# Loading x and the memory also with channels in the partitions, the small vectors as one array, and the plain memory later

## The reference, cut to what matters

```
def rmsnorm(x, g):
    y = x32 * lax.rsqrt(jnp.mean(x32 * x32, axis=-1, keepdims=True) + EPS)
    return (y * g).astype(x.dtype)

mem_n = rmsnorm(mem, norm_mem)
for i in range(DEPTH):                       # DEPTH = 2
    h = rmsnorm(x, norm_mix[i])
    mkv = mem_n @ w_mem_kv[i]                # keys | values of the memory
    proj = h @ w_in_a[li]                    # i = 0: q | k | v | qm
    y_tok = windowed_gqa(q, k, v, sink_a[li])        # i = 0
    y_mem = memory_attn(qm, mk, mv)
    x = x + jnp.concatenate([y_tok, y_mem], axis=-1) @ w_out[i]
    h = rmsnorm(x, norm_ffn[i])
    gu = h @ w_gate_up[i]
    x = x + (silu(gu[..., :D_FF]) * gu[..., D_FF:]) @ w_down[i]
```

## Time and profile before

| | us |
|---|---|
| median of 3 runs (lowest to highest) | 1098.73 (1098.53 to 1102.89) |
| the profiled execution | 1095.95 |
| its span (first to last instruction) | 1094.2 |
| TensorE matmul busy in the span | 1035.4 (95%) |
| VectorE busy | 738.4 (67%) |
| ScalarE busy | 585.7 (54%) |
| GpSimd busy | 117.0 (11%) |

### The profile page before, as it was taken

One profiled execution on the slowest core, in us unless ns is written; L12 is line 12 of the kernel. 1 busy time (PEld: TensorE's weight loads), 2 busy tenths in 40 slices (PEclk: granted clock), 3 DMA queues, 4 the chain that ended last, 5 costly groups with the idle time before them and its releaser, 6 DMA issues.

```text
span 1094.2 us, 13575 instructions
## 1 busy us (share of the span) xinstructions
PE 1035.4 (95%) x5224; PEld 857.8 (78%) x5224; DVE 738.4 (67%) x985; ACT 585.7 (54%) x834; POOL 117.0 (11%) x161
## 2 busy tenths in 40 slices
PE   6997899999999989899999999997989999999996
PEld 5876778789888777788888777886777788888885
DVE  4667774666446577578888766679776766777753
ACT  5557663444345567544443454576656466666641
POOL 1013121000000022200000011013540000000001
PEclk9998999999999999999999989999999999999998
DMA  9655369755565431389989786535365526564541
GB/s 335 202 155 86 106 199 263 244 176 180 166 210 187 152 124 44 114 304 351 353 324 327 288 303 212 164 120 173 125 226 188 183 91 206 178 198 164 171 138 38
DMA packets 98112, 212.42 MB, mean 194 GB/s; under 512 B 5681, under 2 KB 13313, under 8 KB 94657
## 3 DMA queue, kind: packets, MB, share of 16 engines
q1 hardware_dynamic: 93313, 194.46, 52.7%
q0 software_dynamic: 4576, 17.03, 6.4%
q10 hardware_dynamic: 160, 0.07, 0.0%
HBM read 206.82 MB, written 6.15 MB: 195 GB/s over the span
## 4 chain that ended last, share of the span: by engine, by line
PE 67%; DVE 12%; ACT 8%; DMA 5%; issue 5%; POOL 1%; SPq 1%; DVEq 0%; ACTq 0%; POOLq 0%
PE bank L867 20%; PE bank L869 20%; PE bank L868 20%; ACT hi L1191 4%; DVE lo L1619 4%; PE bank L845 3%; DMA raw<-in_w_gate_up 3%; PE bank L881 1%; PE bank L847 1%; DMA raw<-in_w_down 1%; DVE early L1450 1%; DMA raw<-in_w_in 1%; DVE xres L1493 1%; DMA small<-in_sink_a 1%; DVE big L1631 1%
## 5 line engine op out<-in xcount | busy, mean ns | idle before, releaser
L1619 DVE TENSOR_TENSOR lo<-raw,hi 128x2048 fp32r<-128x2048 f32 (+1 forms) x164 | 367.1, 2242 | 220.1 <-ACT hi L1191 219.1
L1191 ACT ACTIVATE hi<-raw 128x2048 fp32r<-128x2048 f32 (+1 forms) x164 | 303.3, 1853 | 191.9 <-PE bank L869 138.5
L867 PE MATMUL bank<-hi,xTh 128*128 128x512 f32 (+2 forms) x896 | 344.9, 385 | 3.5 <-DVE lo L1619 3.4
L869 PE MATMUL bank<-hi,xTl 128*128 128x512 f32 (+2 forms) x896 | 336.3, 375 | 0.0
L868 PE MATMUL bank<-lo,xTh 128*128 128x512 f32 (+2 forms) x896 | 336.1, 375 | 0.0
L867 PEld LDWEIGHTS bank<-hi,xTh 128*128 128x128 f32 x896 | 169.4, 189 | 35.1 <-DVE lo L1619 4.3
L869 PEld LDWEIGHTS bank<-hi,xTl 128*128 128x128 f32 x896 | 169.1, 189 | 31.4
L868 PEld LDWEIGHTS bank<-lo,xTh 128*128 128x128 f32 x896 | 169.5, 189 | 28.2
L867 PE MATMUL bank<-hi,hTh 128*128 128x512 f32 x264 | 103.5, 392 | 0.7 <-DVE lo L1619 0.7
L869 PE MATMUL bank<-hi,hTl 128*128 128x512 f32 x264 | 102.8, 389 | 0.0
L868 PE MATMUL bank<-lo,hTh 128*128 128x512 f32 x264 | 102.8, 389 | 0.0
(11 more groups left out here) (353 smaller groups left out, 1352.8 us busy)
## 6 DMA issues: line engine op xcount, KB each, us to landing
raw<-in_w_gate_up SPq DMA_DIRECT2D x44, 1024.0 KB, 5.7
raw<-in_w_down SPq DMA_DIRECT2D x30, 1024.0 KB, 5.1
raw<-in_w_ada SPq DMA_DIRECT2D x24, 1024.0 KB, 6.6
raw<-in_w_up SPq DMA_DIRECT2D x22, 1024.0 KB, 5.2
raw<-in_w_in SPq DMA_DIRECT2D x21, 1024.0 KB, 5.0
raw<-in_w_out SPq DMA_DIRECT2D x12, 1024.0 KB, 5.1
raw<-in_w_in_b SPq DMA_DIRECT2D x10, 1024.0 KB, 5.1
raw<-in_w_in_a SPq DMA_DIRECT2D x6, 1024.0 KB, 9.9
```

The costliest lines, as they stand in the source:

```text
L867: e.matmul(o, sh, h[:, k, :], start=p.first and k == 0, stop=False)
L869: done = e.matmul(o, sl, h[:, k, :], start=False, stop=p.last and k == p.nk - 1)
L1191: e.activation(hi_s[m % SPLITS][:, 0:n], raw[p.at % RAWS][:, 0:n], ACT.Copy).then_inc(hi_made, 1)
L1619: e.tensor_tensor(lo_s[s][:, 0:n], raw[p.at % RAWS][:, 0:n], hi_s[s][:, 0:n].bitcast(F), ALU.subtract).then_inc(lo_made, 1)
```

## The change

The host hands over three more arrays: `memT` and `xT`, the memory and x with channels in the partitions, and `vectors`, one array of 128 partitions by 330 numbers that holds all gains, taps, offsets, the sink logits and the slopes as columns. The rows, the gain's turn and the 8 turns of memory and x by PE are gone; ACT and DVE make `memTh`, `memTl`, `xTh` and `xTl` straight from the loaded arrays. The plain memory and the plain x are still loaded, since the squares (and later the residual) need them with tokens in the partitions. The plain memory is loaded into `xres` after the sixth weight load. The plain x goes into the same buffer and is issued by POOL behind the root of the memory's squares; the table `const` is issued there too. Both sets of squares stand behind the splits of x. The evacuation of the first `mem` tile becomes a task `late` that waits in the list, so that it comes one tile later, right before that of `vm`.

```
-MIX_TILES = [[(1024, 4, 2), (512, 4, 1), (0, 0, 1)], ...
+MIX_TILES = [[(1024, 4, [2, 2, 1]), (512, 4, [2, 2, 1]), (0, 0, 1)], ...
@@ linear
-            if p == parts - 1:
+            if p == parts - 1 and (kind, l) == ("mem", 0):
+                self.later.append(("late", t))
+            elif p == parts - 1:
                 self.evacuate(t)
@@ run
-        self.put("memgain")
         for k in range(0, 8, 2):
+            self.put("memx", k)
             self.split_through(min(k // 2, SPLITS - 1))
-            self.put("memx", k)
-        self.later.append(("memsq",))
-        self.later.append(("rows",))
-        self.later.append(("relload",))
-        for j in range(2):
-            self.pieces(0, j)
-        self.linear("mem", 0, 0, 512, len(FIRST), "mem", 2)
+        self.later.extend([("rows",), ("relload",), ("xin", 0, 0), ("xin", 0, 2), ("xin", 0, 4), ("xin", 0, 6), ("memsq",), ("sq", 0, 0), ("sq", 0, 1)])
+        self.linear("mem", 0, 0, 512, len(FIRST), "mem", [2, 1, 1, 1])
@@ ScalarE, step memx
-                    e.wait_ge(x_full, filled(step))
-                    e.wait_ge(*emptied(("memgain",)))
+                    if k == 0:
+                        e.wait_ge(d_vec, 16)
+                    e.wait_ge(d_memT[min(k // 2, 2)], 16)
                     for j in range(2):
-                        e.activation(memTh[:, k + j, :], x_bank(step)[...], ACT.Copy, scale=memgain[...])
+                        e.activation(memTh[:, k + j, :], memT[:, k + j, :], ACT.Copy, scale=col(4)[...])
@@ GpSimd
-            e.dma_start(const[:, 128:1408], a["constants"][:, 128:1408]).then_inc(d_const, 16)
-            e.dma_start(steep, a["constants"][:, 1408:1414]).then_inc(d_const, 16)
             for step in order.steps:
                 if kind == "memsq":
                     root(0, 1)
+                    e.dma_start(xres[:, :, :], a["x"][0].rearrange("(t p) d -> p t d", p=128)).then_inc(d_x, 16)
+                    e.dma_start(const[:, 128:1408], a["constants"][:, 128:1408]).then_inc(d_const, 16)
@@ SyncE
-            (memory, 4 weight loads, 16 small loads, x, then the other weights)
+            e.dma_start(memT[:, 0:2, :], a["memT"][:, 0:2, :]).then_inc(d_memT[0], 16)
+            next_load(0)
+            next_load(1)
+            e.dma_start(memT[:, 2:4, :], a["memT"][:, 2:4, :]).then_inc(d_memT[1], 16)
+            next_load(2)
+            e.dma_start(memT[:, 4:8, :], a["memT"][:, 4:8, :]).then_inc(d_memT[2], 16)
+            next_load(3)
+            e.dma_start(xT[:, 0:4, :], a["xT"][:, 0:4, :]).then_inc(d_xT[0], 16)
+            next_load(4)
+            e.dma_start(xT[:, 4:8, :], a["xT"][:, 4:8, :]).then_inc(d_xT[1], 16)
+            next_load(5)
+            e.dma_start(xres[:, :, :], a["mem"][0].rearrange("(t p) d -> p t d", p=128)).then_inc(d_mem, 16)
+            for i in range(6, len(plan)):
+                next_load(i)
```

More of the change, by code:

```diff
@@ L187, in put @@
         kind = task[0]
-        if kind in ("memgain", "rows", "rel", "columns"):
+        if kind in ("rel", "columns"):
             self.turn(task, ON_D)
@@ L248, in put @@
             self.made |= {("merged", k), ("merged", k + 1)}
+        elif kind == "late":
+            return self.evacuate(task[1])
         elif kind == "cv":
@@ L665, in build @@
             p_slots[0] = [[sb(f"p{n}0{i}", [128, 2, 256], R, sc)[:, :, :] for n in "hl"] for i in range(2)]
-        rows = early[:, 2048:2432].rearrange("p (n d) -> p n d", n=3)
-        memx = early[:, 0:2048].rearrange("p (t d) -> p t d", t=2)
-        memrow = early[0:8, 2432:2560]
+        memT = early[:, 0:2048].rearrange("p (k t) -> p k t", k=8)
+        xT = nrm[:, :, :].rearrange("p t (k n) -> p (t k) n", k=4)
         mstage = [early[:, 2560 + 512 * l:3072 + 512 * l].rearrange("p (t d) -> p t d", t=2) for l in range(2)]
@@ L771, in ready @@
             what, l = source
+            if what == "in" and l == 0:
+                return in_low, k // 2 + 1
             if what == "in":
@@ L931, in tensor_program @@
                     matmuls(parts[name[0]], name[1])
[L932 to L945, removed]
+                elif kind == "xin" and name[0]:
                     s, k = name
[L947 to L950, removed]
+                    e.wait_ge(acc_dve, order.res_at[s, k // 4])
                     turned(claim(step), blocks_of(xres, k * 128, 2))
                 elif kind == "mk":
+                    e.wait_ge(d_ident, 16)
                     t_ = order.tile_of["mem", name[0], 0]
@@ L1207, in scalar_program @@
                     gain = col((0, 2, 1, 3)[s])
-                    e.wait_ge(x_full, filled(step))
-                    e.wait_ge(*emptied(("rows",)))
+                    if s:
+                        e.wait_ge(x_full, filled(step))
+                    else:
+                        e.wait_ge(d_xT[k // 4], 16)
                     for j in range(2):
-                        e.activation(xTh[:, k + j, :], x_bank(step)[:, j * 256:(j + 1) * 256], ACT.Copy, scale=gain[:, k + j:k + j + 1]).then_inc(x_high, 1)
+                        view = x_bank(step)[:, j * 256:(j + 1) * 256] if s else xT[:, k + j, :]
+                        e.activation(xTh[:, k + j, :], view, ACT.Copy, scale=gain[:, k + j:k + j + 1]).then_inc(x_high, 1)
                 elif kind == "sq":
@@ L1654, in vector_program @@
                     gain = col((0, 2, 1, 3)[s])
-                    if s == 0 and k == 0:
-                        e.wait_ge(*emptied(("rows",)))
                     e.wait_ge(x_high, order.high_at[step])
                     for j in range(2):
-                        done = e.scalar_tensor_tensor(out=xTl[:, k + j, :], in0=x_bank(step)[:, j * 256:(j + 1) * 256], scalar=gain[:, k + j:k + j + 1],
+                        view = x_bank(step)[:, j * 256:(j + 1) * 256] if s else xT[:, k + j, :]
+                        done = e.scalar_tensor_tensor(out=xTl[:, k + j, :], in0=view, scalar=gain[:, k + j:k + j + 1],
                                                       in1=xTh[:, k + j, :].bitcast(F), op0=ALU.mult, op1=ALU.subtract)
-                    done.then_inc(x_dve, 1)
+                    done.then_inc(x_dve if s else in_low, 1)
                 elif kind == "sq":
@@ L1892, in gpsimd_program @@
                 elif kind == "relload":
-                    e.wait_ge(x_full, filled(("rows",)))
                     e.dma_start(rel, a["rel_bias_2"]).then_inc(d_rel, 16)
@@ L2048, in shape_constants @@
         c[:, 896 + 256 * t:1152 + 256 * t] = np.where(key[None, :] <= q[:, None], 0.0, -BIG)
-    c[:, 1408:1414] = [[0.125 * 2.0 ** (8.0 * (2 * k + (i >= 64) + 1) / 12) for k in range(6)] for i in range(128)]
     col, kcol = p % 64, key % 64
@@ L2054, in shape_constants, with vectors_of, turned_blocks @@
     return c
+def vectors_of(a):
+    rows = [a[n].reshape(-1, 128) for n in ("norm_mix", "norm_ffn", "norm_mem", "g_mix_2", "g_ffn_2", "c_2", "conv_rnn_w_2", "conv_rnn_b_2",
+                                            "b_rg_2", "b_ig_2", "lru_lambda_2")]
+    taps = a["conv_ffn_w_2"].reshape(-1, 128)
+    rows += [taps[0:88], a["b_in_2"][0, 2376:3400].reshape(-1, 128), taps[88:132], a["conv_ffn_b_2"].reshape(-1, 128)]
+    steep = [[0.125 * 2.0 ** (8.0 * (2 * k + (i >= 64) + 1) / 12) for k in range(6)] for i in range(128)]
+    sink = np.broadcast_to(a["sink_a"].reshape(1, 12), (128, 12))
+    return np.ascontiguousarray(np.concatenate([np.concatenate(rows).T, sink, steep], axis=1).astype(np.float32))
+def turned_blocks(x):
+    return np.ascontiguousarray(x[0].T.reshape(8, 128, 256).transpose(1, 0, 2))
 def distance_buckets():
@@ L2076 @@
     given["constants"] = shape_constants()
+    given["vectors"] = vectors_of(given)
+    given["xT"], given["memT"] = turned_blocks(given["x"]), turned_blocks(given["mem"])
     given["onehot"] = distance_buckets()
+    for name in ("norm_mix", "norm_ffn", "norm_mem", "g_mix_2", "g_ffn_2", "c_2", "conv_rnn_w_2", "conv_rnn_b_2", "b_rg_2", "b_ig_2", "lru_lambda_2",
+                 "conv_ffn_w_2", "conv_ffn_b_2", "sink_a"):
+        del given[name]
     for name, v in given.items():
```

84 lines of the change are left out of this document (30 added, 54 removed).

## The result

The changed kernel takes 1106.44 us (median of 7 runs, 1105.63 to 1111.15); the kernel before, run beside it, 1098.73. The ratio is 1.0086, 95% interval 1.0065 to 1.0107: 0.86% slower, against a forecast of 1106 and "slower". This ratio is not the quotient of the two medians, which is 1.0070: the medians are 7.7 us apart, the ratio stands for 9.4 us (7.1 to 11.8). The profiled execution is 1107.79 with a span of 1105.9.

What follows compares the result with a forecast made beforehand. PE, busy for 95% of the span, was taken to bound the kernel. Second scores 8.4 us late, plus 1.4, less 2.3, made 7.5 us; on the median of 1098.73 that gave 1106, range 1103 to 1109 (8 in 10: 1098 to 1111).

Steps and rivals of the forecast that it cites:

- The start: PE's first weight matmul: at about 7.6 us instead of 10.96, with the stop until 16.70 gone.
- Feeding: Weight landings up to part 6: memory tile ends at 22.1, part 5 waits 2.5 us, PE about 6.5 us ahead.
- The added wait: Before the keys' turn: the chain through x's load leaves PE idle from 38.5 to 51.0 but for one turn.
- The clock: After PE's pause: next turns and 12 matmuls at the low pace, 6.0 us instead of 3.2, until 57.0.
- short wait: Rival at x's load: x lands in 5.1 us, not 7.5, and the clock stays high; about 1101; chance 0.23.
- Back to today's places: From first scores onward: second scores at 69.8, 8.4 us late; net 7.5 late after part 11, kept to the end.
- near 69: Sign that the forecast is right, on PE: the second scores come near 69 us.
- The total: Whole kernel: 7.5 us late, 1106 on the median of 1098.73; slower by over 0.5% given 0.60.
- Lead kept: Rival at the memory's keys: x arrives before PE asks, so the start's lead stays, 7.4 us less, 1091; chance 0.11.

Runs made afterwards that it cites:

- e4: The changed kernel, but GpSimd loads x, waits until it has landed and loads it again, the squares waiting for both; ratio to the kernel before 1.0107.
- e3: The changed kernel with 42 more 128x512 matmuls, their product unused, ahead of the turn of the keys; ratio to the kernel before 1.0074.
- e11: The kernel before with only the small vectors as one array, run a second time with more rounds; ratio to the kernel before 0.9989.
- e9: The changed kernel with own plain-memory buffer, early SP load of x, x's squares right behind part 6's split, turns and scores later; 1091.85 us, ratio 0.9951.
- e1: The changed kernel with an own buffer for the plain memory, SP loading plain x behind the seventh weight load; ratio to the kernel before 0.9997.

## Why the prediction was right

*The start.* First matmul 8.43, forecast 7.6. The missing 0.8 us is a term that I left out: ScalarE's table load, 1.28 us, stood ahead of its first instruction (the data themselves were there 0.5 us sooner than the 5.2 that I took). Before, it ran early and cost nothing; after, it stands behind the wait for the first data. Before, then after:

```profile
1.83 1.28 ACT L1191 ACT_TABLE_LOAD   x1 [1.83 <-issue]
```

```profile
4.65 1.28 ACT L1187 ACT_TABLE_LOAD   x1 [4.65 <-DMA early<-in_memT]
```

A first instruction that waits is not enough for this: before, it too waited for its weights, until 8.46. After, ScalarE's program has two waits ahead of it, for the vectors and for `memT`; no run takes them apart. The 0.8 us did not matter, but only just: part 3's weights landed at about 12.75 and ScalarE was done with what stands ahead of their split at 12.74. The end of the tile: forecast 22.1, measured 22.7.

*Feeding.* Wait in part 5 forecast 2.5, measured 1.44; 108 matmuls done at 38.5 and 38.1. Part 6's weights landed at 26.05, forecast 26.7.

*The added wait.* x issued 33.6 and 32.87, in use 41.1 and 40.94; keys turned 48.8 and 48.65; queries 51.0 and 50.91. The time of x's load, chosen at 7.5 between 5.1 and 8.4, was 8.0. The estimate by the Trainium skill (DMA: Bandwidth & Descriptors, sections Anatomy of one DMA and Queues, rings and completion order), 4.4 us for a load alone and 6.8 beside an equal one, lies below what was measured with several loads in flight, 8.0. The second of e4's two loads, issued at 41.15 when little else was in flight, was in use at 46.47, 5.3 us later, where the estimate for a load alone is 4.4.

*The clock.* This step failed in its worth. The low clock came as forecast (nine matmuls 0.43 us apart, 51.65 to 55.2), but it was charged 2.8 us, in the sum and in the rival "short wait", and is worth about 0.3 us by itself (e3): I had written that VectorE has the queries by then, at 56.4 or so, without seeing that this is a second chain of almost equal length. The 57.9 of the forecast is the end of the first scores, 0.9 us behind their start at 57.0; they started at 56.31.

*Back to today's places.* 168 matmuls and the second scores done at about 69.4, forecast 69.8, so 8.0 us late for a forecast of 8.4. I put the second scores behind the 168th matmul ("near 69"), where the kernel before has them; they stand behind the 156th (65.64). The sum does not feel that, since the stretch holds 48 matmuls and one more set of scores either way. The first biased pass came at 92.25, 6.9 us later than the earlier trace rows, forecast 7.5; the landmark 7.3; the medians differ by 7.7.

*The total.* That 1106.44 meets 1106 so closely is in part luck. The forecast put 7.5 us on the kernel before, and the ratio says 9.4, with 7.5 near the lower end of its interval; the two medians met because that of the kernel before was 1098.73 here, where its other runs had 1097.1 to 1098.2. The chain up to the landmark was right to some tenths. The rest has the size of the 1.9 us that are open (e11).

*Lead kept.* The rival's direction was right: once the chain ends before TensorE asks, the lead stays (e9). Its price is neither confirmed nor excluded. 1091 stands close to e9's 1091.85, but that was beside a kernel before of 1097.68; the ratio gives 5.4 us for a price of 7.4, and its interval ends at 7.6. The landmark's lead is 7.4, by other terms: e9 has no wait in part 5, for which the rival took off 2.5 us, and its turns stand behind 120 matmuls and not 108, so the chain had until 39.4 and not 34.

## What to carry to other kernels

A buffer shared by two loads ties the second load to the last reader of the first; in an in-order queue, all behind its user then waits for a DMA. When a start is made faster, follow the first instruction that needs a late side product, here a row factor, and count the waits in the queue between it and TensorE, not only the work. And before a slow clock is charged, look for the second chain that ends with it.

## What the runs showed of the hardware

- TensorE's granted clock fell to 0.50 within a wait of 10.4 us (0.94 from 40 to 42, 0.50 from 42 on), and equally in e1 with waits of 1.22 and 1.64 us and a few turns between (0.50 from 42 to 48). In e3, with waits of 0.80 and 1.63 us around the same turns but 42 matmuls straight ahead of them, it stayed at 1.00, and so it did behind e9's single wait of 1.11 us.
- The same kernel can be granted 0.79 in one execution and 1.00 in another over the same 15 us in mid-program. The stretch of some 240 us around it took 241.7 us in one execution of that kernel and 239.3 in the other, and 238.2 to 241.9 over all thirteen profiles. Differences of that size between two profiles are settled by landmarks ahead of such a stretch, or by medians.
- A 1 MB load from GpSimd took 7.6 to 9.6 us with weights in flight, and 5.3 at most with little else in flight (the second one of e4). Issuing the 640 KB that GpSimd had put behind it later changed that by 0.4 us at most.
